# A four-layer network on one core: dilated attention outputs done for two heads together on both halves of the array, gates from a tanh, and two smaller moves

## The reference, cut to what matters

```python
# dilated attention: 24 heads of 64, three groups of 8 with dilation 1, 4, 16; head h of the output
# is the softmax-weighted sum over heads h, 8 + h and 16 + h, then gated
wts = jax.nn.softmax(jnp.stack(lses, axis=0), axis=0)
o = jnp.sum(wts[..., None] * jnp.stack(outs, axis=0), axis=0)
o = o.reshape(Bsz, S, DIL_OUT) * jax.nn.silu(g.astype(jnp.float32))
mixed = jnp.concatenate([y.astype(jnp.float32), o], axis=-1).astype(x.dtype)
return x + jnp.einsum("bsf,fd->bsd", mixed, w_out.astype(x.dtype))
...
# block attention: 16 heads of 64 over 256 tokens (one block, so plain causal attention), gated
o = moba_attention(q, k, v).reshape(Bsz, S, MOBA_WIDTH) * jax.nn.silu(g.astype(jnp.float32))
return x + jnp.einsum("bsf,fd->bsd", o.astype(x.dtype), w_out.astype(x.dtype))
...
# mixer, compression of keys and values
flat = jnp.moveaxis(blocks, 3, 2).reshape(b, -1, g, CMP_BLOCK * d)
return jax.nn.gelu(flat @ w1 + b1) @ w2
```

## Time and profile before

| | us |
|---|---|
| median of 3 runs (1836.48 to 1838.0) | 1837.55 |
| the profiled execution, its own time | 1838.62 |
| its span, first to last instruction | 1836.8 |
| TensorE busy (share of the span) | 1773.5 (97%) |
| VectorE busy | 1177.1 (64%) |
| ScalarE busy | 902.0 (49%) |

### The profile page before, as it was taken

One profiled execution on the slowest core, in us unless ns is written; L12 is line 12 of the kernel. 1 busy time (PEld: TensorE's weight loads), 2 busy tenths in 40 slices (PEclk: granted clock), 3 DMA queues, 4 the chain that ended last, 5 costly groups with the idle time before them and its releaser, 6 DMA issues.

```text
span 1836.8 us, 30394 instructions
## 1 busy us (share of the span) xinstructions
PE 1773.5 (97%) x11896; PEld 1581.4 (86%) x11896; DVE 1177.1 (64%) x2153; ACT 902.0 (49%) x1419; POOL 18.6 (1%) x20
## 2 busy tenths in 40 slices
PE   6999999999999999999999999999989999999988
PEld 6999899988799989999799989799979888777876
DVE  6555477667755566555675678555577894684764
ACT  4444354665544445443546664434455554453564
POOL 1000000000000000000000000000000000000000
PEclk9999999999999999999999999999999998799999
DMA  7555455534455554454446344545535443104421
GB/s 291 188 182 195 172 196 188 225 138 181 164 188 190 182 194 180 177 196 181 183 173 252 138 173 148 197 178 199 199 132 185 159 164 125 69 1 172 175 104 55
DMA packets 29908, 311.70 MB, mean 170 GB/s; under 512 B 3313, under 2 KB 3697, under 8 KB 4849
## 3 DMA queue, kind: packets, MB, share of 16 engines
q1 hardware_dynamic: 28944, 307.18, 45.1%
q0 software_dynamic: 864, 3.15, 0.5%
HBM read 309.26 MB, written 1.05 MB: 169 GB/s over the span
## 4 chain that ended last, share of the span: by engine, by line
PE 84%; DVE 7%; ACT 4%; issue 2%; DMA 2%; SPq 0%; DVEq 0%; ACTq 0%
PE psum L862 81%; PE psum L869 3%; DMA ring<-in_weights 2%; DVE ring_r L495 1%; ACT region_r L489 1%; ACT Sb L1786 1%; DVE Sb L2311 1%; DVE PTs L2427 0%; DVE xs L2210 0%; ACT Sb L1680 0%; DVE x L2214 0%; DVE xs L2174 0%; DVE region L2539 0%; DVE xs_r L501 0%; DVE xs L2158 0%
## 5 line engine op out<-in xcount | busy, mean ns | idle before, releaser
L495 DVE TENSOR_TENSOR ring_r<-ring,region_r 128x1024 fp32r<-128x1024 f32 x487 | 582.2, 1220 | 191.4 <-ACT region_r L489 189.8
L489 ACT ACTIVATE region_r<-ring 128x1024 fp32r<-128x1024 f32 x495 | 516.0, 1055 | 379.9 <-PE psum L862 351.3
L862 PE MATMUL psum<-hH,region_r 128*128 128x256 f32 x2256 | 556.5, 285 | 5.0 <-DVE PTs L2427 3.1
L862 PE MATMUL psum<-xs_r,region_r 128*128 128x256 f32 x2240 | 544.3, 282 | 0.0
L862 PEld LDWEIGHTS psum<-hH,region_r 128*128 128x128 f32 x2256 | 425.0, 188 | 18.6 <-issue 9.5
L862 PEld LDWEIGHTS psum<-xs_r,region_r 128*128 128x128 f32 x2240 | 422.4, 189 | 4.8 <-issue 0.5
L862 PE MATMUL psum<-hH,ring_r 128*128 128x256 f32 x2336 | 315.2, 277 | 0.0
L862 PE MATMUL psum<-region_r 128*128 128x512 f32 (+1 forms) x944 | 305.0, 389 | 2.7 <-DVE region_r L2252 2.1
L862 PEld LDWEIGHTS psum<-hH,ring_r 128*128 128x128 f32 x2336 | 290.5, 188 | 0.0
L862 PEld LDWEIGHTS psum<-region_r 128*128 128x128 f32 (+1 forms) x944 | 173.7, 185 | 39.6 <-DVE region_r L2252 2.6
L862 PE MATMUL psum<-region_r,hH 128*128 128x512 f32 (+3 forms) x544 | 176.2, 360 | 10.8 <-DVE xs_r L501 6.0
(11 more groups left out here) (240 smaller groups left out, 1712.1 us busy)
## 6 DMA issues: line engine op xcount, KB each, us to landing
ring<-in_weights SPq DMA_DIRECT2D x192, 1536.0 KB, 6.4
gpost<-in_posts POOLq DMA_DIRECT2D x6, 512.0 KB, 5.0
cst<-in_const SPq DMA_DIRECT2D x1, 1213.0 KB, 23.1
xs<-in_mem SPq DMA_DIRECT2D x1, 1024.0 KB, 5.6
x<-in_x SPq DMA_DIRECT2D x1, 1024.0 KB, 8.1
out<-x SPq DMA_DIRECT2D x2, 512.0 KB, 2.7
pars<-in_par SPq DMA_DIRECT2D x1, 368.0 KB, 6.1
p<-in_par SPq DMA_DIRECT2D x1, 206.0 KB, 23.1
```

What stands on the lines that cost most here:

```text
L489: eng.activation(unit.high, unit.raw, ACT.Copy).then_inc(h_ready, 1)
L495: eng.tensor_tensor(unit.low, unit.raw, unit.high.bitcast(F32), ALU.subtract).then_inc(l_ready, 1)
L862: ins = pe.matmul(bank, lhsT, rhs, start=start, stop=stop)
```

## The change

Six edits.

1. The query and key weights of the dilated layer are packed by unit (`by_head`), so branch b of unit s lies in half (3 s + b) % 2. Branches 0 and 1 of a unit are then in opposite halves of the partitions, and their scores are issued alternating.
2. The dilated outputs of units 0 and 1, 2 and 3, 4 and 5, 6 and 7 are done together by `halves_outputs`, 12 products alternating between the halves of the output partitions, in steps 4, 6, 8 and 10, after the scores of branches 0 and 1 and in front of the turned tiles. They were done one unit in each step from 3 to 10, at the step's end.
3. MoBA's gate is made as x/2 (1 + tanh(x/2)): ScalarE takes tanh straight from the bank, VectorE adds one and multiplies by the bank (an added instruction for each of eight tiles), and the missing factor of a half is a second operation in the division of MoBA's probabilities. The three silu lots and their table loads go.
4. VectorE's later weight splits of MoBA move by a step or half a step.
5. In the mixers VectorE's split of kc and vc moves behind the next two tiles (qm 0, qm 1).
6. The gates' banks are freed by VectorE, a step later than by ScalarE's copy.

```diff
@@ TensorE, scores @@
+                    if kind == "dil" and 0 in branches:
+                        jobs = [Job("S", tag, s, b) for b in range(2)]
+                        for job in jobs:
+                            job.wait_empty(pe)
+                        for n in range(NT):
+                            for b, job in enumerate(jobs):
...
+                                mm(to, q_of(s, b)[:, n, :], k_of(s, b) if n else k_of(s, b)[:, 0, :], True, True,
+                                   job.full if n else None)
+                        return
@@ TensorE, outputs @@
+                def halves_outputs(pair):
+
+                    todo = []
+                    for s in pair:
+                        job = Job("PV", tag, s)
+                        job.wait_empty(pe)
+                        half = out_half(units[s])
+                        for b in range(BRANCHES["dil"]):
+                            Job("PT", tag, s, b).wait_emptied(pe)
+                            pt = PTs[:, s % 2, b * 384:]
+                            v0, v1 = v_of(s, b)
+                            todo.append((2 * b, job, job.bank[half, 0:SEQ], v0, pt[:, 0:SEQ]))
+                            todo.append((2 * b + 1, job, job.bank[half, P:SEQ], v1, pt[:, SEQ:3 * P]))
+                    for n, job, o, v, p in sorted(todo, key=lambda one: one[0]):
+                        mm(o, v, p, n == 0, n == 5, job.full if n == 5 else None)
...
+                        if tag == "dil" and some.start == 0 and s > lag and (s - lag) % 2 == 0:
+                            halves_outputs((s - lag - 2, s - lag - 1))
                         if 0 <= s - lag < len(units):
                             turns(s - lag, [b for b in some if b < BRANCHES[units[s - lag][0]]])
-                    if s > lag:
+                    if s > lag and tag != "dil":
                         outputs(s - lag - 1)
...
-                      lambda s, b: head_tile(0, 4 * b + s // 2, s % 2),
-                      lambda s, b: head_tile(1, 4 * b + s // 2, s % 2),
+                      lambda s, b: head_tile(0, *divmod(3 * s + b, 2)),
+                      lambda s, b: head_tile(1, *divmod(3 * s + b, 2)),
@@ ScalarE, MoBA gates @@
-                    copy(job, ogT[:, s, :], job.bank[:, 0:SEQ])
-                if s in OG_SILU:
-                    a, b = OG_SILU[s]
-                    for t in range(a, b):
-                        Job("og", t).wait_emptied(act_)
-                    act_.activation(ogT[:, a:b, :], ogT[:, a:b, :], ACT.Silu).then_inc(og_ready, 1)
+                    job.wait_full(act_)
+                    act_.activation(ogT[:, s, :], job.bank[:, 0:SEQ], ACT.Tanh, scale=0.5).then_inc(og_ready, 1)
@@ VectorE, attention @@
+                        if kind == "moba":
+                            ins = dve.tensor_scalar(p, p, r[:, c:c + 1], 0.5, ALU.mult, ALU.mult)
@@ VectorE, mixer @@
-                        job.wait_emptied(dve)
+                    elif kind == "qm" and at < 2:
+                        c = at
+                        Job("kc" if c == 0 else "vc", 0).wait_emptied(dve)
                         own.settle()
@@ VectorE, MoBA @@
             def gate_lows(s):
-                if s + 4 < N_OA:
-                    odd_lows(28 + s, 29 + s)
-                if 5 <= s <= 8:
-                    for n in (2 * s - 10, 2 * s - 9):
+                if 1 <= s <= N_OA:
+                    job = Job("og", s - 1)
+                    dve.wait_ge(og_ready, s)
+                    dve.scalar_tensor_tensor(ogT[:, s - 1, :], ogT[:, s - 1, :], 1.0, job.bank[:, 0:SEQ],
+                                             ALU.add, ALU.mult).then_inc(job.free, 1)
+                    if s + 3 < N_OA:
+                        odd_lows(27 + s, 28 + s)
+                if 5 <= s <= 9:
+                    for n in range(max(2 * s - 11, 0), min(2 * s - 9, N_OO)):
                         low_part(dve, U_OO + n)
```

More of the change, by code:

```diff
@@ L222 @@
 BRANCHES = {"nsa": 2, "mem": 1, "dil": 3, "moba": 2}
-OG_SILU = {2: (0, 3), 5: (3, 6), 7: (6, 8)}
 def output_of(units, s):
@@ L1077, in scores @@
                         return
+                    if kind == "dil" and 0 in branches:
[4 more added lines that the diff above has]
+                            for b, job in enumerate(jobs):
+                                to = job.bank[:, n * P:P + n * SEQ]
+                                if n:
+                                    to = to.rearrange("p (i t) -> p i t", i=NT)
+                                mm(to, q_of(s, b)[:, n, :], k_of(s, b) if n else k_of(s, b)[:, 0, :], True, True,
+                                   job.full if n else None)
+                        return
                     for b in branches:
@@ L2339, in back @@
                         p = scores_of(kind, s)[:, u:v]
-                        ins = dve.tensor_scalar(p, p, r[:, c:c + 1], None, ALU.mult)
+                        if kind == "moba":
+                            ins = dve.tensor_scalar(p, p, r[:, c:c + 1], 0.5, ALU.mult, ALU.mult)
+                        else:
+                            ins = dve.tensor_scalar(p, p, r[:, c:c + 1], None, ALU.mult)
                         if n == len(todo) - 1:
@@ L2965, in odd_out @@
                 _, p, _ = unit
-                dve.wait_ge(og_ready, 1 + sum(p >= b for _, b in OG_SILU.values()))
+                Job("og", p).wait_emptied(dve)
                 dve.tensor_tensor(odd_mixedT[:, p, :], job.bank[:, 0:SEQ], ogT[:, p, :], ALU.mult).then_inc(job.free, 1)
             def gate_lows(s):
-                if s + 4 < N_OA:
-                    odd_lows(28 + s, 29 + s)
-                if 5 <= s <= 8:
-                    for n in (2 * s - 10, 2 * s - 9):
+                if 1 <= s <= N_OA:
[7 more added lines that the diff above has]
+                    for n in range(max(2 * s - 11, 0), min(2 * s - 9, N_OO)):
                         low_part(dve, U_OO + n)
@@ L3107, in tail_chunks @@
     xbc0, dt0, q0 = D, 3 * D, 3 * D + SSD_H
+    by_head = np.arange(3 * 512).reshape(3, 8, HD).transpose(1, 0, 2).reshape(-1)
+    w = w[:, np.r_[0:q0, q0 + by_head, q0 + 1536 + by_head, q0 + 3072:w.shape[1]]]
     k0, v0, g0 = q0 + 1536, q0 + 3072, q0 + 4608
```

## The result

The changed kernel takes 1840.30 us (median of 20 runs, 1834.39 to 1844.35), the kernel before on the same chip 1836.82 us (20 runs, 1833.42 to 1840.22). The ratio is 1.0019, 95% interval 1.0012 to 1.0027: slower by 3.5 us, where 4.9 us faster was forecast.

A forecast was written before the change was run, and what follows sets the result against it. TensorE, busy 97% of the span, was taken as the bound. Mixers -2.1, MoBA -10.0, dilated +4.1 at full clock and +3.1 for clock falls sum to -4.9 us: median 1837.55 becomes 1832.7, range 1823 to 1839.5.

The forecast's parts named there:

- two falls' worth, +3.1 us: Dilated attention: new idle stretches drop TensorE's clock to 1.2 GHz, priced as two MoBA falls of 1.6 us each.
- +4.1 at full clock: Dilated attention: the stage gets 4.1 us longer at full clock, although TensorE has 13.6 us less to do.
- about 9: Dilated attention: upper bound in us of the clock's cost, when every product on the path is slow; lower bound none.
- The third rival: Dilated stage at 1.2 GHz from step 4 to its end: +15 us there, total +3, 1840.5 us; chance 0.07.
- The wait ahead of the outputs: Dilated attention: TensorE idles 2.5 us before joined outputs, until ScalarE's copy of branch 2, behind exponentials and high part.
- the order of readies: Dilated attention: ends of VectorE's line 2322, one per unit, come 8 and 5.4 us apart in turn.
- The paired scores: Dilated attention: scores of branches 0 and 1 in opposite halves take 0.65 us less, eight times, 5.2 us.
- Overlap of halves: Dilated outputs: opposite halves overlap fully, two units in 2.1 us instead of 4.2, saving 8.4; alternation adds nothing.
- MoBA: First scores to final product: 51.5 us becomes 41.1, gaining 10.4, of which 7.3 waits and 3.1 half clock.
- The division's second operation: MoBA's probabilities on VectorE: no row prices it; taken as none, at most 0.5 us a unit.
- 0.4 for late splits: Final product behind MoBA: VectorE is later relative to TensorE, leaving -10.0 us in all from the 10.4 gain.
- The mixers: TensorE's wait for vc's bank shrinks by 1.0 us in each of two layers: -2.1 us.

The follow-up runs named there:

- filled: Changed kernel plus extra TensorE products, results unused, in the idle places of the dilated stage, waits untouched: 1831.37 us.
- pair_only: Kernel before with edit 1 alone (weights packed by unit, scores of branches 0 and 1 in pairs): 1834.55 us, before 1836.40.
- copy_first: Changed kernel with ScalarE's copy of branch 2 of the turned tiles ahead of the same step's exponentials, in attention stages with three branches: 1825.07 us.
- unit_by_unit: Changed kernel with each joined group's twelve products issued unit by unit, six to one half then six to the other, instead of alternating: 1842.90 us.
- dil_only: Kernel before with edits 1 and 2 alone (packed weights, paired scores, joined outputs): 1847.45 us, before 1837.22.
- gate7: Changed kernel with MoBA's last output gate done in step 7, ahead of the weight splits, instead of step 8: 1835.53 us, before 1837.60.

## Why the prediction was wrong

**The step that failed** is "two falls' worth, +3.1 us" for the clock in the dilated stage. The stage became 11.6 us longer (forecast +7.2), which leaves 7.5 for the clock beside the +4.1 at full clock. The forecast had weighed it from single long waits in MoBA, each followed by 3.42 us at 1.2 GHz. Here the clock, already low up to step 4, stayed low for 23.9 us instead of 17.1 and then fell three times more, for 6.8, 6.8 and, up to the stage's end, 5.6 us: 43 us of the stage ran at 1.2, and all four output groups lay wholly or largely in it. TensorE was busy for 33.7 us of these 43, against 16.2 of 17.1 before; half of the difference, 8.7 us, is an estimate of what the lower clock added, near the 7.5. The bound of "about 9" was right; the place within it was not. The third rival, "the clock stays down", had the mechanism and, with +3 in total, nearly the time (partly by luck: it had +15 in the stage, where 11.6 were measured, and counted on 2.1 from the mixers and the whole gain of MoBA); it was given 0.07.

The Trainium skill ("TensorE: Matmul & The Clock Gate", "Loop structure matters more than you think") says that the loop nest decides whether products stay at the full clock, and contrasts products back to back with a long DMA wait between every two. The direction agrees: `filled`, with its gaps filled by products, is 9 us faster. But no long wait was needed: the longest in this stage is 2.43 us, and 43 of 71 us ran at 1.2 GHz.

**The wait ahead of the outputs** was right in its cause, with the releaser and the chain as written, and a little long: 1.7 us (steps 4 and 6), 2.4 and 2.2, where 2.5 was written. So was the order of readies; `filled` confirms 8.0 and 5.5.

**The paired scores** were taken as 5.2 us of relief. In `pair_only` TensorE's busy time in the stage fell by 4.7 us, near the term, but the stage only by 2.3 and the kernel by 1.9, as the idle time grew.

**Overlap of halves**: right for the alternating group, 2.1 us for 24 passes at 2.4 GHz (`copy_first`). Wrong in that the joining would do without the alternation. MoBA's 0.80 us came from halves of only four passes each; `unit_by_unit` shows that the overlap reaches four passes and no further. The Trainium skill (same page, Part 3, "The mechanism") states that products start and end strictly in program order. For groups of twelve, what the forecast had drawn from this rule (only neighbours overlap) was the better guess; the four pairs at the switch of units are not in line with it.

**MoBA**: -10.4 forecast from first scores to final product, -10.7 measured, all waits but 0.14 us gone (in `dil_only`, which lacks these edits, 7.6 us of idle time remain). The division's second operation, which had no price in the forecast's rows, cost nothing: 0.348 against 0.346 us for 128x256. Behind it the forecast allowed 0.4 for late splits; the rows show 2.3, from another cause: the bank of the last gate. Edit 6 stood in the list of edits, and the question of who waits for a bank that is freed a step later was asked for the gates and not for the first bank behind them. `gate7` settles it.

**The mixers**: the wait shrank by the forecast 1.0 us in each layer. In the kernel's time it was -2.6 alone and nothing that could be measured beside the dilated edits.

**The sum**: dilated 4.4 us too low, behind MoBA 1.9 too low, the mixers' 2.1 us of gain not found, and MoBA 0.3 better than forecast. That makes 8.1; the miss is 8.4 us (3.5 slower against 4.9 faster).

## What to carry to other kernels

Price a new wait on TensorE by what runs behind it at half clock, not by its length: here putting another engine's copy ahead of one instruction of 0.94 us, in the steps that have it, was worth 10 us, and dummy products in the gaps 9 us. When work moves forward in one queue, look at the queue that feeds it and move the feeding instruction too; the copy ahead of the exponentials gave back 15 us. When a bank is freed later, look past its own ring for the first other use of that bank.

## What the runs showed of the hardware

Products into opposite halves of the output partitions overlap fully when alternated (24 passes in 2.1 us, where twelve passes into one half alone take 2.1), but of twelve passes to one half and twelve to the other only four and four overlapped. Waits of at most 2.4 us left TensorE's clock at 1.2 GHz for 43 of 71 us. The same instructions ahead of the dilated stage took 1575.8 to 1583.7 us in 13 profiles, so that single profiles of this kernel can only be compared stage by stage, and even a stage depends on where the clock stands: with the joined outputs the dilated stage was 71.15 to 71.21 us in five profiles and 70.67 in a sixth, and with the early copy 62.98 in one and 65.99 in another.
